# A trunk layer and four transformer layers on one core: projection tiles in the drain, a modulation behind the last expert, and fused FFN norm operations

## What is computed

```python
def modulate(h, shift, scale):
    return h * (1.0 + scale) + shift

# first block, with g1, sh2, sc2, g2 from silu(c) @ w_ada + b_ada
x = x + g1 * mix_out(fx, attn_x, conv_x, w_fourier, w_out)     # concat of the three @ w_out
hx2 = rms_norm(x, norm2) * (1 + sc2) + sh2
x = x + g2 * hier_moe(hx2, ...)                                # top-1 group, top-2 experts in it
x = rms_norm(x, norm_final)

# each of the four layers, with its own shifts, scales and gates from silu(c_2) @ ada_w_2[i] + ada_b_2[i]
x = x + gate_a * attention(modulate(rms_norm(x, gain_a), shift_a, scale_a))
x = x + gate_f * ffn(modulate(rms_norm(x, gain_f), shift_f, scale_f))
```

## Time and profile before

| | |
|---|---|
| median of the runs | 2264.11 us |
| the profiled execution | 2259.81 us, span 2257.9 us, mean granted clock 0.958 |
| TensorE busy | 2019.3 us, 89% of the span |
| DVE busy | 733.6 us, 32% |
| ACT busy | 665.2 us, 29% |
| transfers | 552.18 MB, mean 245 GB/s |
| last attention pair and projection | 194.5 to 243.1 us |
| norm 2 and routing, up to the first expert | 243.1 to 284.1 us |
| experts | 284.1 to 751.9 us |
| layer 0 from its group rows to the end | 771.2 to 2257.9 us, all layers |

### The profile page before, as it was taken

One profiled execution on the slowest core, in us unless ns is written; L12 is line 12 of the kernel. 1 busy time (PEld: TensorE's weight loads), 2 busy tenths in 40 slices (PEclk: granted clock), 3 DMA queues, 4 the chain that ended last, 5 costly groups with the idle time before them and its releaser, 6 DMA issues.

```text
span 2257.9 us, 39143 instructions
## 1 busy us (share of the span) xinstructions
PE 2019.3 (89%) x16974; PEld 1701.7 (75%) x16974; DVE 733.6 (32%) x1333; ACT 665.2 (29%) x1202; POOL 33.1 (1%) x53
## 2 busy tenths in 40 slices
PE   6997977677677799999999999998799999999999
PEld 4786744334444588899987789997579998878999
DVE  1132210111111122344534434543534452224454
ACT  3111200000000333434433243443433443324343
POOL 1000000000000000000000000000000000000000
PEclk8998899989999899999999999999899999999999
DMA  9554799999999625644662554565175466333443
GB/s 384 217 230 186 282 398 426 428 428 428 428 428 428 279 111 194 270 168 158 264 243 93 219 228 187 190 240 220 69 278 203 166 245 246 112 112 131 180 153 134
DMA packets 41000, 552.18 MB, mean 245 GB/s; under 512 B 4544, under 2 KB 4928, under 8 KB 5056
## 3 DMA queue, kind: packets, MB, share of 16 engines
q1 hardware_dynamic: 33984, 449.98, 50.2%
q0 software_dynamic: 6912, 100.67, 10.9%
HBM read 549.58 MB, written 1.05 MB: 244 GB/s over the span
## 4 chain that ended last, share of the span: by engine, by line
PE 72%; DMA 17%; ACT 5%; DVE 4%; issue 1%; SPq 0%; DVEq 0%
PE bank L398 33%; DMA ring<-in_moe 17%; PE bank L385 16%; PE bank L392 5%; PE bank L436 4%; PE bank L637 3%; PE bank L377 2%; PE bank L421 1%; PE bank L448 1%; ACT hT L986 1%; PE bank L818 1%; ACT xsq_parts L988 1%; DMA ring<-in_ada_head 1%; PE bank L734 1%; ACT work L1144 1%
## 5 line engine op out<-in xcount | busy, mean ns | idle before, releaser
L398 PE MATMUL bank<-xsq_parts,ring_parts 128*128 128x256 f32 x1408 | 398.9, 283 | 0.0
L398 PEld LDWEIGHTS bank<-xsq_parts,ring_parts 128*128 128x128 f32 x1408 | 270.8, 192 | 0.0
L385 PE MATMUL bank<-hT,ring 128*128 128x256 f32 x1024 | 234.2, 387 | 2.5 <-DVE mod L1414 1.8
L637 PE MATMUL bank<-ring,xsq 128*32 128x256 f32 x2048 | 145.4, 432 | 97.4 <-DMA ring<-in_moe 96.7
L385 PEld LDWEIGHTS bank<-hT,ring 128*128 128x128 f32 x1024 | 193.9, 192 | 36.2 <-issue 7.7
L398 PE MATMUL bank<-xsq_parts,mixT_parts 128*128 128x256 f32 x704 | 202.2, 287 | 8.7 <-DVE hT_parts L1739 8.5
L963 ACT CAST mixT_parts<-ring 128x1024 fp32r<-128x1024 f32 (+1 forms) x152 | 151.7, 1003 | 185.8 <-PE bank L398 185.8
L398 PE MATMUL bank<-hT_parts,mixT_parts 128*128 128x256 f32 x704 | 199.7, 284 | 0.0
L398 PE MATMUL bank<-xsq_parts,xn_parts 128*128 128x256 f32 x704 | 199.2, 283 | 0.0
L398 PE MATMUL bank<-hT_parts,xn_parts 128*128 128x256 f32 x704 | 199.2, 283 | 0.0
L637 PEld LDWEIGHTS bank<-ring,xsq 128*32 128x32 f32 x2048 | 66.7, 121 | 171.0 <-DMA ring<-in_moe 126.7
(11 more groups left out here) (297 smaller groups left out, 3222.2 us busy)
## 6 DMA issues: line engine op xcount, KB each, us to landing
ring<-in_moe SPq DMA_DIRECT2D x96, 2048.0 KB, 12.5
ada_ring<-in_ada POOLq DMA_DIRECT2D x48, 2048.0 KB, 12.2
ring<-in_gu SPq DMA_DIRECT2D x44, 2048.0 KB, 7.8
ring<-in_down SPq DMA_DIRECT2D x32, 1408.0 KB, 6.0
ring<-in_pair SPq DMA_DIRECT2D x24, 1536.0 KB, 6.5
ring<-in_na SPq DMA_DIRECT2D x12, 2048.0 KB, 9.5
ring<-in_out SPq DMA_DIRECT2D x10, 2048.0 KB, 7.8
ring<-in_ada_head SPq DMA_DIRECT2D x3, 2048.0 KB, 14.9
```

Source lines behind the costliest of these rows:

```text
L385: m = mm(dst, w[:, k, lo:lo + P], h[:, k, :], start=k == 0, stop=k == KT - 1)
L398: m = mm(dst, w[a], x[b], start=start and (a, b) == (0, 0), stop=stop and a == 1)
L637: m = mm(bank[0][CAP * q:CAP * (q + 1), 0:T], xg[:, 4 * c + k, h * CAP:(h + 1) * CAP], w[:, k, q * T:(q + 1) * T], start=(c, k) == (0, 0), ...
```

## The change

Three things change. First, the output tiles of out_0 are no longer done one after another behind the last pair: a function `mix_out` does part of one tile's sum, over the mixT tiles in an order that puts the last pair's output (tile 5) last. Four tiles get seven of their eight matmuls before the last pair's transposes, two more behind them, then the eighth for all six, then two tiles in full. They take banks of their own, and DVE's updates follow that order. Second, group 1's modulation leaves the routing: its rows go behind the experts, its copies behind the squares of norm 3, its columns behind norm 3's sum and its `take_mods` behind `normalise(3)`. Third, in the FFN norm DVE multiplies x by gain and 1/rms in one fused operation, ACT adds the shift once, rounded, and DVE gets the low part from xn, shift and high part in a second fused operation; ACT's splits 2 and 3 of the first weights now wait for `h_lo`. The count x0 of `h_ready` follows from the tiles that are no longer written to hT.

```diff
@@ tensor engine
+            MIX_TILES = ((0, 0), (0, T), (2, 0), (2, T), (1, 0), (1, T), (6, 0), (7, 0))
+            MIX_ORDER = (0, 1, 6, 7, 2, 3, 4, 5)
+
+            def mix_out(d, k0, k1):
+
+                n = FIRST["out_0"] + d // 4
+                if d % 4 == 0 and k0 == 0:
+                    wait_chunk(pe, n)
+                b, at = MIX_TILES[d]
+                for k in MIX_ORDER[k0:k1]:
+                    m = mm(bank[b][:, at:at + T], chunk3(n, 512)[:, k, d % 4 * P:(d % 4 + 1) * P], mixT[:, k, :],
+                           start=k == MIX_ORDER[0] and at == 0, stop=k == MIX_ORDER[-1], skip_group_check=True)
+                return m
...
+                if last:
+                    pe.wait_ge(na["ada_ready"], NA_PAIRS)
+                    pe.wait_ge(na["o_ready"], NA_PAIRS - 1)
+                    for d in range(4):
+                        mix_out(d, 0, KT - 1)
                 if not first:
                     pe.wait_ge(na["p_ready"], j)
...
+                if last:
+                    pe.wait_ge(na["v_ready"], j)
+                    for d in range(4, 6):
+                        mix_out(d, 0, KT - 1)
                 if not first:
                     pe.wait_ge(na["pt_act"], j)
...
-            out_proj("out_0")
+            for d in range(6):
+                m = mix_out(d, KT - 1, KT)
+                if d % 2:
+                    m.then_inc(used[FIRST["out_0"] % RING] if d == 3 else y_done, 1)
+            for d in range(6, KT):
+                mix_out(d, 0, KT).then_inc(used[(FIRST["out_0"] + 1) % RING] if d == 7 else y_done, 1)
...
                 group_columns(0, "norm2")
-                pe.wait_ge(mods_taken, 1)
-                group_rows(1, "route")
...
-                group_columns(1, "route")
 
                 pe.wait_ge(zeroed, 1)
-                pe.wait_ge(mods_taken, 2)
+                pe.wait_ge(mods_taken, 1)
...
                 moe_branches(pe, expert, packed, turn_comb)
+                group_rows(1, "final")
                 norm(3)
+                group_columns(1, "final")
@@ scalar engine
                 for k in range(KT):
                     act.wait_ge(xn_ready, KT * e + k + 1)
-                    A(out_t[:, k, :], xn[:, k, :], ACT.Identity, scale=g(k), bias=shift(k)).then_inc(h_ready, 1)
                     if high is not None:
-                        A(part["xsq"][:, k, :], xn[:, k, :], ACT.Identity, scale=g(k), bias=shift(k)).then_inc(h_hi, 1)
+                        A(part["xsq"][:, k, :], xn[:, k, :], ACT.Identity, bias=shift(k)).then_inc(h_hi, 1)
+                    else:
+                        A(out_t[:, k, :], xn[:, k, :], ACT.Identity, scale=g(k), bias=shift(k)).then_inc(h_ready, 1)
...
-                act.wait_ge(h_hi, KT * (i + 1))
                 for f in range(2, 4):
+                    act.wait_ge(h_lo, KT * i + 4 * (f - 1))
                     split(0, 0, f)
@@ vector engine
+            def normalise_split(e, before, g, shift):
+
+                def scaled(k):
+                    V.scalar_tensor_tensor(xn[:, k, :], xT[:, k, :], gain[:, g, k:k + 1], rinv[:, :], ALU.mult, ALU.mult).then_inc(xn_ready, 1)
+
+                dve.wait_ge(rinv_ready, e + 1)
+                for k in range(3):
+                    scaled(k)
+                for k in range(KT):
+                    dve.wait_ge(h_hi, before + k + 1)
+                    V.scalar_tensor_tensor(part["hT"][:, k, :], xn[:, k, :], mod[:, shift + k:shift + k + 1], part["xsq"][:, k, :].bitcast(F32),
+                                           ALU.add, ALU.subtract).then_inc(h_lo, 1)
+                    if k + 3 < KT:
+                        scaled(k + 3)
...
-                normalise(5 + 2 * i)
-                for k in range(KT):
-                    dve.wait_ge(h_hi, KT * i + k + 1)
-                    V.tensor_tensor(part["hT"][:, k, :], hT[:, k, :], part["xsq"][:, k, :].bitcast(F32), ALU.subtract).then_inc(h_lo, 1)
+                normalise_split(5 + 2 * i, KT * i, 2, 3 * KT)
```

More of the change, by code:

```diff
@@ L290, in build @@
                   "ffn": ((6, 0), (6, T), (7, 0), (7, T)), "down": ((4, 0), (4, T), (0, 0), (0, T)),
-                  "norm2": ((1, 0), (1, T), (2, 0), (2, T)), "route": ((2, 0), (2, T), (3, 0), (3, T))}
+                  "norm2": ((1, 0), (1, T), (2, 0), (2, T)), "final": ((0, 0), (0, T), (1, 0), (1, T))}
         def group_bank(place, c):
@@ L713, in _ @@
                 group_rows(4 * i + 2, "attn")
-                x0 = KT * (4 + 2 * i)
+                x0 = KT * (4 + i)
                 n0 = FIRST.get(f"pair_{i}")
@@ L1078, in _ @@
                 m.then_inc(tok_act, 1)
-                group_out(1, "route")
                 n0 = FIRST["moe"]
@@ L1103, in _ @@
                 log_exp_tables()
-                norm(3, xT, (x_done, KT, 1), xT, lambda k: vc("normf", k, 1), lambda k: cst("zero"))
+                norm(3, xT, (x_done, KT, 1), xT, lambda k: vc("normf", k, 1), lambda k: cst("zero"), lambda: group_out(1, "final"))
             for i in layers:
@@ L1307, in normalise @@
                     V.tensor_tensor(xn[:, k, :], xT[:, k, :], rinv[:, :], ALU.mult).then_inc(xn_ready, 1)
+            def normalise_split(e, before, g, shift):
[10 more added lines that the diff above has]
+                        scaled(k + 3)
+            MIX_DONE = 3
             def update(c, f, n, a, g):
                 if f < 3:
-                    dve.wait_ge(y_done, 6 * a + 3 * c + f + 1)
+                    dve.wait_ge(y_done, MIX_DONE + 6 * (a - 1) + 3 * c + f + 1)
                 else:
@@ L1404, in _ @@
             V.scalar_tensor_tensor(gain[:, 2, :], mod[:, 4 * KT:5 * KT], 1.0, vc("norm2"), ALU.add, ALU.mult).then_inc(mods_ready, 1)
-            for c in range(2):
-                for f in range(4):
-                    update(c, f, FIRST["out_0"] + c, 0, 2)
+            for d, (b, at) in enumerate(((0, 0), (0, T), (2, 0), (2, T), (1, 0), (1, T), (6, 0), (7, 0))):
+                if d == 2 or d == 7:
+                    wait_used(dve, FIRST["out_0"] + d // 4)
+                elif d in (0, 4, 6):
+                    dve.wait_ge(y_done, d // 2 if d else 1)
+                V.scalar_tensor_tensor(xT[:, d, :], bank[b][:, at:at + T], mod[:, 2 * KT + d:2 * KT + d + 1], xT[:, d, :],
+                                       ALU.mult, ALU.add).then_inc(x_done, 1)
             def take_mods(g, place):
@@ L1481, in _ @@
                 then(V.tensor_scalar(pos, R(1), -1.0, None, ALU.add), "route")
-                take_mods(1, "route")
                 n0 = FIRST["moe"]
@@ L1540, in _ @@
                 normalise(3)
+                take_mods(1, "final")
             for i in layers:
```

## The result

The changed kernel takes 2237.24 us (median of 4 runs, 2232.39 to 2239.21); the kernel before, run beside it, 2261.94 (4 runs, 2258.71 to 2268.96). The ratio is 0.9881, with a 95% interval of 0.9855 to 0.9907, which stands for 21 to 33 us. That is 24.7 us less by the medians; the profiled spans, 2257.9 and 2237.2, differ by 20.7.

The account below looks back on a forecast made before the run. TensorE's order of work bounds the kernel, except the transfer-bound expert stage, where only the start counts, and gaps waiting for ACT and DVE. 15.4 + 10.0 - 3.0 + 8.9 = 31.3 us gained: median 2232.8 us, range 2224 to 2246.

Parts of the forecast that it names:

- Part 1: Drain of the last attention pair: output projection matmuls fill TensorE's idle time before the transposes; gain 15.4 us, bounds 11.7 to 16.
- the old gap: TensorE idle 10.24 us, 194.5 to 204.8, awaiting the last pair's softmax; forecast filled with matmuls at granted clock 1.00.
- The lower bound of 11.7: Drain: gain in us if the last pair's transposes and value product stay at the half clock.
- The rival of a late out_0 chunk: Drain: first out_0 chunk takes 20.7 us, projection fill starts 8.8 us late, clock falls again; 2245.3 us, chance 0.08.
- Part 2: Routing: without group 1's modulation rows, rank and clearing products run earlier and the gather starts 10.0 us sooner; bounds 8.4 to 11.9.
- Part 3: Behind the last expert: 96 row matmuls now precede the norm's sum; loss 3.0 us, bounds 2.0 to 6.6.
- I take 6.0, from 752.4 on: Behind the last scatter: 96 row matmuls take 6.0 us, between 5.39 at full clock and 7.83 begun at half.
- the margin of the group 2 loads: Behind the experts: last group 2 load lands at 773, TensorE needs it at 777.8; free by nearly 5 us.
- the moved modulation comes back on the path: Rival behind the experts: half clock for rows and sums plus a last group 2 load wait; 10 to 12 us, chance 0.12.
- Part 4: FFN norm of each layer: fused DVE operations at 0.40 us ready the eighth tile sooner; gain 8.9 us, bounds 4.8 to 10.0.
- The clock rival: TensorE-bound stretches, about 1600 us: denser order lowers granted clock; 2% costs 32 us, 3% gives 2281; chance 0.04, half slower.

## Why the prediction was right, and where it was wrong

**The bound.** The reading held: TensorE's order of work set the time outside the experts. (The slices at 426 to 428 GB/s in the earlier trace rows are the seventh to thirteenth; the sixth has 398.) The expert stage kept its length but for 1.9 us (465.8 against 467.7), of which 1.6 is the last down product at the full clock (1.93 us against 3.54). No stretch turned out to be bound by something else.

**Part 1** was forecast at 15.4 and gave 15.4, each term within 0.2 us, with the clock at 1.00 in the old gap. The lower bound of 11.7 guarded against a clock that stays low, and wasn't needed on the after side; on the before side the undone part showed that 2 us of the gain hang on how long the old gap's low clock lasts. The rival of a late out_0 chunk fell: no wait in the drain.

**Part 2** was forecast at 10.0 and gave 9.5. The clearing products were sized right (5.40 for 5.37); the rest is the rank products, 2.2 us at the half clock where I had 1.6 and a short wait, and the logits (4.71 us, 4.40 before).

**Part 3** is the step that failed, by its size: "I take 6.0, from 752.4 on". The start of the rows was put 0.55 us behind the scatter, and it was 3.28; a second wait of 1.66 us stood in the middle; and the rows, sized between 5.39 and 7.83 us, took 9.7 because the first wait had brought the clock down. The loss was 11.2 where I had 3.0, and 6.6 at worst. The row that could have warned stands in the earlier trace rows: TensorE idle 1.77 us behind the scatter, charged to ACT. I read that wait as ACT's alone. The square was done 0.56 us before TensorE went on, and the packet on the instruction queue at 751.1 is as far ahead of it as in the other kernels: TensorE had no code there either, and moving the rows ahead of ACT's wait brought out what lay under it. The experiments show two things of it. The wait hangs on the place behind the experts: it moves to the norm when the rows leave. And part of it is contention with weight transfers: the two waits together are 2.6 us with the loads held, 4.6 to 5.4 with SP's queue running. That both waits are for code is argued from the packets' constant distance, not shown by an experiment, and whether the jump over the branch that isn't run makes the code late is untested. The other step of this part, the margin of the group 2 loads, was right.

The rival "the moved modulation comes back on the path", at 10 to 12 us and 2241, had the right size and half the right reason: the half clock was there for rows, though not for the sums, and the wait was for code, not for the last load. Its chance of 0.12 was too low, since the forecast's own bound left out any wait behind the experts.

**Part 4** was forecast at 8.9 and gave 9.0. The pace of 0.40 us for a fused operation, taken from two in a row rather than from a lone one (0.48), was the right row to use. That is the norm's own stretch; by the medians undoing the part costs 4.4 us, half of it. The estimate by the Trainium skill, "VectorE: DVE Perf Modes", the section on the TRN2 errata, was 0.33 us; the trace shows 0.40, and the measurement decides.

**The clock rival** (a denser order costs clock everywhere, slower than before) fell: the mean granted clock is 0.96 in both kernels. A mild relative of it showed in one stage, 4.0 us with the stage's code unchanged; that is why the spans differ by 20.7 where the stretches of the table give 24.6.

**The sum**: 31.3, less 8.2 in part 3, less 0.5 in part 2, plus 1.9 in the experts and 0.1 in part 4, is 24.6; with the third layer's attention it is the 20.7 of the spans. For the profiled run the forecast was 2228.5, and it took 2239.21, 10.7 more. By the medians the miss is only 4.4, and that is luck: the forecast put the median 4.3 us above the profiled run, and it lies 2.0 below. Taken by itself the moving of the rows (parts 2 and 3) brought nothing, and nearly the whole gain is the drain's and the FFN norms'. Undone one at a time, the three parts are worth about 14, -1 and 4.5 us by the ratios, 17 together, where all of them give 25. Each ratio has an interval of about 4 us either way, so the rest isn't clear of noise, and it isn't explained. Of the 11.2 us lost behind the experts the place in the last expert pair gives back 7.2, for 0.7 us more in the experts.

## What to carry to other kernels

The first code behind a large block of control flow (here the experts with a branch that isn't run) isn't free to start: look there for waits by "issue" and for packets on the instruction queue, also under a wait that is charged to another engine, and price a block moved to that place with them and with the half clock that follows. To find such a case, compare the end of what the wait is charged to with the start of the waiting engine. A small block of matmuls belongs into waits for weights ahead of that place, where the clock is up; here the move behind the experts was worth nothing, and the move into the last pair 4 us by the medians (2232.13 against 2236.09 without a move; the intervals overlap). And differences of some 4 us between kernels of this length can come from the moment at which an untouched stage starts, so a part's worth is read from its own stretch, between two marks, rather than from the totals.

## What the runs showed of the hardware

- Behind the experts single packets of 0.02 MB came on the instruction queue, and TensorE went on 2.2 to 2.8 us after each in every profile; that they are its code is the reading of this constant distance. With SP's loads running the two waits together were 4.6 to 5.4 us, with the transfers held 2.6. Idle transfer engines let the first packet leave 2.7 to 2.8 us sooner, in each of two pairs of kernels.
- After a wait of 3.28 us the granted clock was 0.50 up to 736 us and the 96 matmuls took 9.7 us; after one of 0.76 us it was 1.00 and they took 6.0.
- The same 100 us of instructions ran at a clock of 0.94, 0.92 or 0.89, and in 102.5, 104.1 or 106.4 us; two executions of one kernel agreed within 0.15 us.
- DVE's fused product and sum of 256 elements, one behind the other, came every 0.40 us; the plain product's 0.34 was not reached.
